# A decoder layer on one core: gaps of 128 and 256 bytes behind the two halves of the split activations

## The chip, the cores and the metric

One Trainium2 chip, one of its cores. The metric is the device time of one execution in microseconds; the time before is the median of three executions.

## The reference

One decoder layer on 256 tokens of width 2048, all in float32:

```
h = rms_norm(x); proj = h @ w_in                     # 2048 x 13312
o_da  = differential attention (8 heads), o_ret = retention (8 heads)
o_mem = cross-attention into 256 memory tokens (w_mem_kv: 2048 x 2048)
merged = sum_b sigmoid(gate_b) * (o_b @ w_o_b)       # 3 x 1024 x 2048
x = x + merged @ w_out                               # 2048 x 2048
hf = rms_norm(x)
x = x + (silu(hf @ w_ffn_gate) * (hf @ w_ffn_up)) @ w_ffn_down   # width 5632
```

## The kernel before, in words

Nearly all of the work is in matrix products, and each product runs as three passes on TensorE. Every float32 operand is split into a high part, rounded to the type fp32r, and a low part, the remainder, kept in fp32r too; the product is hi x hi, hi x lo and lo x hi, added up in PSUM. The activations are the stationary operand (a tile of 128 rows by 128 tokens, so 512 bytes in each partition), and the weights are the moving operand (512 columns, so 2048 bytes in each partition). For every pass the stationary tile is loaded anew, since TensorE's weight load belongs to each matmul. In the code:

```
for n, (a, w) in enumerate(((hi, w_hi), (hi, w_lo), (lo, w_hi))):
    e = pe.matmul(dst, a[:, k0 + k, tok], w[:, s % RING, k, :], ...)
```

That is line 1582 (`three_passes`), which the projections, the branches and the output projection use. Lines 1664 to 1666 (`product`) are the same three passes for the feed-forward part and for the blocks that run with seven products in place of eight.

The stationary tiles live in a few places:

- `hT_hi` and `hT_lo`, 16 x 256 float32 per partition (16,384 bytes each), hold the two halves of the transposed normed residual stream. They serve the input projection, the three branch gates, the gate and up projections of the feed-forward part, and, in four of their columns, its last down projection.
- `oT_hi` and `oT_lo`, as large, hold the memory tokens, then the branch outputs, then the merged rows.
- `aT_hi` and `aT_lo` hold the gated activations of a feed-forward block; `cmb_hi`, `cmb_lo`, `r_cmb` and `p_cmb` hold sums of activation blocks for the seven-product form.

The moving tiles are `w_hi` and `w_lo` (a ring of four slots), and in the feed-forward part `f_hi`, `f_raw` (whose remainder view is named `f_raw_rest`), and `sum`.

SBUF is handed out in the order of the declarations, each tensor right behind the one before it. Ahead of the activations stand the small tables, with a pad `align` of 32 bytes as the last of them. Then come `hT_hi`, `hT_lo`, `raw`, `w_hi`, `w_lo` and all other large tiles. Every size from `hT_hi` to the last is a multiple of 512 bytes per partition, so all these tiles start at one and the same place modulo 512: in the kernel before, the distance between any stationary tile and any moving tile that it meets is 0 modulo 512. The tile `ident`, the moving operand of the transposes (line 1604, `turn`), stands among the small tables; from it to `hT_hi` it is 256 bytes modulo 512.

The order of the work is written out by hand for each engine. SP loads the weights into `raw` or `f_raw`, ScalarE (line 507, and 847 to 857) makes the high part, VectorE (line 929, and 1427 to 1440) the low part, and TensorE multiplies. TensorE waits for semaphores that VectorE raises (`lo_done`, `part_lo`). TensorE's stream of passes is broken at some places by transposes and by the small attention products in plain float32 (lines 1642 and 1657, 128 x 256 moving columns).

Of the kernel before, what the change touches and what calls it, by code (L numbers as in the profile page):

```python
# [33 lines left out]
P = 128  # L34
# [28 lines left out]
UNIT_PART = (0, 1, 3, 5, 7, 8, 10, 12, 14, 15, 16, 17)  # L63
PARTS, UNITS, SLOTS, RAWS, SUMS, NS = 18, 12, 5, 5, 3, 6
ALIGN = 8
SUM_PART = (2, 4, 6, 9, 11, 13)
N0, S0W, S0T, S1W, S1T, S2W, S2T, N1, S3W, S3T, S4W, S4T, S5W, S5T, D0, D1, D2, D3 = range(PARTS)
RB_KIND = ("nnSnSnSn", "nSnSSnSn")
# [21 lines left out]
def program(nc, x, mem, positions, w_in, da_q_norm_g, da_k_norm_g, da_lambda_q1, da_lambda_k1,  # L90
# [6 lines left out]
    with ExitStack() as ctx:  # L97
        def sb(name, shape, dt=F32):
            return ctx.enter_context(nc.sbuf_tensor(name, shape, dt))
# [33 lines left out]
        lrden = sb("lrden", [P, 2, 2])  # L133
        sb("align", [P, ALIGN])
        hT_hi = sb("hT_hi", [P, KD, TOK], F32R)
        hT_lo = sb("hT_lo", [P, KD, TOK], F32R)


        with ExitStack() as mixers:
# [151 lines left out]
        def part(f, p):  # L291

            return (f - 1) * PARTS + p
# [626 lines left out]
        def _(v):  # L920
# [522 lines left out]
            def sum_first(f, i, u):  # L1443
# [4 lines left out]
                if (f - 1) * NS + i >= SUMS:  # L1448
                    e, j = divmod((f - 1) * NS + i - SUMS, NS)
                    v.wait_ge(part_done, part(e + 1, SUM_PART[j]) + 1)  # L1450
                elif i == 2:
# [583 lines left out]
```

## Time and profile before

| what | value |
|---|---|
| runs, median of three | 1628.27 us (1627.23 to 1629.32) |
| span of the profiled execution | 1625.4 us |
| TensorE matmul busy | 1618.2 us, 7373 matmuls |
| TensorE weight load busy | 1339.3 us, 7373 loads |
| VectorE busy | 1271.1 us |
| ScalarE busy | 908.2 us |
| granted TensorE clock | 1.000 (mean) |

The span runs from the first to the last instruction of the profiled execution; for that execution no other time is shown, and the runs' median lies 2.9 us above its span. Matmuls are pipelined, and the busy time of each (some 390 ns) overlaps that of the next, so what a matmul costs is the distance from its start to the next one's start; the chain of work that ended last gives it, as time divided by count.

### The profile page before, as it was taken

The numbers are of one execution on the slowest core, as the hardware profiler recorded it, in microseconds if no ns is written. First come the engines' busy times: TensorE is split into PE (matmuls) and PEld (weight loads), VectorE is DVE, ScalarE is ACT, GpSimd is POOL, SyncE is SP. The second block draws the span as 40 slices with busy tenths as digits, with TensorE's granted clock in tenths as the row PEclk, the third lists the DMA queues.
The fourth block names the chain that finished last, engine by engine and source line by source line (L and its number), as shares of the span: only waits on it lengthen the run. The fifth ranks groups of instructions, "written<-read, shape, count | busy, mean of one in ns | idle before, by whom it ended". The sixth has DMA issues, their size and how long they took to land.

```text
span 1625.4 us, 20227 instructions
## 1 busy us (share of the span) xinstructions
PE 1618.2 (100%) x7373; PEld 1339.3 (82%) x7373; DVE 1271.1 (78%) x1325; ACT 908.2 (56%) x989; POOL 80.6 (5%) x73
## 2 busy tenths in 40 slices
PE   9999999999999999999999999999999999999999
PEld 7888888888888888888888888888888888888887
DVE  5565545589777777777975589999999999999995
ACT  6654454555555554445554465656655665656653
POOL 0000000000011100000000000100100100100101
PEclk9999999999999999999999999999999999999999
DMA  9876555556554555566675756868868868868866
GB/s 339 278 214 194 157 180 175 174 179 220 179 166 162 164 172 168 174 188 199 202 245 182 249 166 207 252 211 248 246 212 250 249 208 249 244 220 240 253 211 178
DMA packets 178007, 341.35 MB, mean 210 GB/s; under 512 B 11793, under 2 KB 16401, under 8 KB 177169
## 3 DMA queue, kind: packets, MB, share of 16 engines
q1 hardware_dynamic: 167056, 319.45, 60.4%
q0 software_dynamic: 10880, 20.97, 7.1%
q8 instruction: 44, 0.72, 0.2%
q14 instruction: 27, 0.21, 0.0%
HBM read 317.31 MB, written 2.10 MB: 197 GB/s over the span
## 4 chain that ended last, share of the span: by engine, by line
PE 90%; issue 6%; DVE 1%; DMA 1%; POOL 1%; ACT 1%; SPq 0%; DVEq 0%; ACTq 0%; POOLq 0%
PE acc L1582 43%; PE at L1664 9%; PE at L1666 9%; PE at L1665 9%; PE acc L1666 5%; PE acc L1664 5%; PE acc L1665 5%; PE at L1582 3%; PE at L1604 2%; POOL rstd L480 1%; PE at L1642 0%; PE at L1657 0%; DMA raw<-in_w_mem_kv 0%; DMA raw<-in_w_in 0%; DVE w_lo L929 0%
## 5 line engine op out<-in xcount | busy, mean ns | idle before, releaser
L929 DVE TENSOR_TENSOR w_lo<-raw,w_hi 128x1024 fp32r<-128x1024 f32 x319 | 386.6, 1222 | 239.6 <-ACT w_hi L507 235.4
L507 ACT ACTIVATE w_hi<-raw 128x1024 fp32r<-128x1024 f32 x319 | 337.1, 1060 | 360.9 <-PE acc L1582 300.3
L1582 PE MATMUL acc<-w_hi,hT_hi 128*128 128x512 f32 x752 | 297.6, 396 | 0.0
L1582 PE MATMUL acc<-w_hi,hT_lo 128*128 128x512 f32 x752 | 293.1, 390 | 0.0
L1582 PE MATMUL acc<-w_lo,hT_hi 128*128 128x512 f32 x752 | 293.0, 390 | 0.0
L857 ACT ACTIVATE f_hi<-sum 128x2048 fp32r<-128x2048 f32 x60 | 115.3, 1922 | 121.2 <-DVE sum L1461 118.0
L1582 PEld LDWEIGHTS acc<-w_hi,hT_hi 128*128 128x128 f32 x752 | 141.2, 188 | 30.9 <-issue 1.3
L1582 PEld LDWEIGHTS acc<-w_hi,hT_lo 128*128 128x128 f32 x752 | 141.2, 188 | 29.7
L1582 PEld LDWEIGHTS acc<-w_lo,hT_hi 128*128 128x128 f32 x752 | 141.3, 188 | 28.4
L1582 PE MATMUL acc<-w_hi,oT_hi 128*128 128x512 f32 x384 | 151.2, 394 | 1.5 <-DVE oT_lo L955 1.4
L1582 PE MATMUL acc<-w_hi,oT_lo 128*128 128x512 f32 x384 | 149.6, 390 | 0.0
L1582 PE MATMUL acc<-w_lo,oT_hi 128*128 128x512 f32 x384 | 149.5, 389 | 0.0
L1427 DVE TENSOR_TENSOR f_raw_rest<-f_raw,f_hi 128x2048 fp32r<-128x2048 f32 x64 | 145.2, 2283 | 4.3 <-ACT f_hi L847 4.3
L1440 DVE TENSOR_TENSOR sum_rest<-sum,f_hi 128x2048 fp32r<-128x2048 f32 x60 | 137.2, 2286 | 3.9 <-ACT f_hi L857 3.9
L1664 PE MATMUL at<-f_hi,aT_hi 128*128 128x512 f32 x320 | 124.7, 390 | 0.1
L1666 PE MATMUL at<-f_hi,aT_lo 128*128 128x512 f32 x320 | 124.7, 390 | 0.0
L1665 PE MATMUL at<-f_raw_rest,aT_hi 128*128 128x512 f32 x320 | 124.6, 389 | 0.0
L847 ACT ACTIVATE f_hi<-f_raw 128x2048 fp32r<-128x2048 f32 x64 | 119.8, 1904 | 0.0
L1664 PE MATMUL acc<-f_hi,hT_hi 128*128 128x512 f32 x280 | 109.9, 393 | 0.0
L1666 PE MATMUL acc<-f_hi,hT_lo 128*128 128x512 f32 x280 | 109.1, 390 | 0.0
L1434 DVE TENSOR_TENSOR f_raw_rest<-f_raw,f_hi 128x1536 fp32r<-128x1536 f32 x60 | 105.2, 1753 | 0.7
L852 ACT ACTIVATE f_hi<-f_raw 128x1536 fp32r<-128x1536 f32 x60 | 88.9, 1481 | 12.6 <-PE acc L1666 9.7
(349 smaller groups left out, 2658.1 us busy)
## 6 DMA issues: line engine op xcount, KB each, us to landing
raw<-in_w_in SPq DMA_DIRECT2D x208, 512.0 KB, 3.8
f_raw<-in_w_ffn_down SPq DMA_DIRECT2D x88, 512.0 KB, 4.8
f_raw<-in_w_ffn_gate SPq DMA_DIRECT2D x80, 512.0 KB, 3.9
f_raw<-in_w_ffn_up SPq DMA_DIRECT2D x80, 512.0 KB, 5.0
proj<-down POOLq DMA_DIRECT2D x40, 512.0 KB, 6.4
raw<-in_w_mem_kv SPq DMA_DIRECT2D x32, 512.0 KB, 6.2
raw<-in_w_out SPq DMA_DIRECT2D x32, 512.0 KB, 3.7
raw<-in_w_o_mem SPq DMA_DIRECT2D x16, 512.0 KB, 5.0
```

The lines of the kernel that those rows point to most:

```text
L507: act.activation(w_hi[:, s % RING], raw[:, s % RING], ACT.Copy).then_inc(hi_done, 1)
L847: act.activation(f_hi[slot(f, p)][:], f_raw[unit(f, u) % RAWS][:], ACT.Copy).then_inc(part_hi, 1)
L852: act.activation(f_hi[slot(f, p)][:, 0:3], f_raw[unit(f, u) % RAWS][:, 1:4], ACT.Copy).then_inc(part_hi, 1)
L857: act.activation(f_hi[slot(f, p)][:], sums[sum_buf(f, i)][:], ACT.Copy).then_inc(part_hi, 1)
L929: v.tensor_tensor(w_lo[:, s % RING], raw[:, s % RING], w_hi[:, s % RING].bitcast(F32), ALU.subtract).then_inc(lo_done, 1)
L1427: v.tensor_tensor(f_rest[r][:], f_raw[r][:], f_hi[slot(f, p)][:].bitcast(F32), ALU.subtract).then_inc(part_lo, 1)
L1434: v.tensor_tensor(f_rest[r][:, 1:4], f_raw[r][:, 1:4], f_hi[slot(f, p)][:, 0:3].bitcast(F32), ALU.subtract).then_inc(part_lo, 1)
L1440: v.tensor_tensor(sums_rest[n][:], sums[n][:], f_hi[slot(f, p)][:].bitcast(F32), ALU.subtract).then_inc(part_lo, 1)
L1582: e = pe.matmul(dst, a[:, k0 + k, tok], w[:, s % RING, k, :], start=first and k == 0 and n == 0, stop=last and k == 1 and n == 2)
L1664: pe.matmul(dst, hi, whi, start=first, stop=False)
L1665: pe.matmul(dst, hi, wlo, start=False, stop=False)
L1666: return pe.matmul(dst, lo, whi, start=False, stop=last)
```

## The change

Two tensors that nothing reads or writes are declared behind `hT_hi` and behind `hT_lo`:

```
+HI_GAP, LO_GAP = 32, 64
...
         sb("align", [P, ALIGN])
         hT_hi = sb("hT_hi", [P, KD, TOK], F32R)
+        sb("hi_gap", [P, HI_GAP])
         hT_lo = sb("hT_lo", [P, KD, TOK], F32R)
+        sb("lo_gap", [P, LO_GAP])
```

They take 128 and 256 bytes in each partition. `hT_hi` stays where it was, `hT_lo` moves up by 128 bytes, and everything declared behind it by 384 bytes. No instruction is added, removed or moved on any engine.

## Rows read from the trace of the kernel before

**Rows 1.** The page: span, and busy time of each engine.
```profile
span 1625.4 us, 20227 instructions
PE 1618.2 (100%) x7373; PEld 1339.3 (82%) x7373; DVE 1271.1 (78%) x1325; ACT 908.2 (56%) x989; POOL 80.6 (5%) x73
PEclk9999999999999999999999999999999999999999
```
**Rows 2.** The page: chain that ended last; and TensorE's clock over the core.
```profile
PE 90%; issue 6%; DVE 1%; DMA 1%; POOL 1%; ACT 1%; SPq 0%; DVEq 0%; ACTq 0%; POOLq 0%
...
core 0: 1625.4 us, clock 1.000
```
**Rows 3.** The chain in order of time: start us, us, what, xcount.
```profile
19.92 70.27 PE acc L1582 x310
...
99.94 46.24 PE acc L1582 x204
...
157.04 1.73 PE at L1642 x8
...
174.59 24.50 PE acc L1582 x108
...
954.85 22.67 PE acc L1582 x100
```
**Rows 4.** Groups by line and tiles, TensorE: xcount | busy us, mean ns.
```profile
L1582 PE MATMUL acc<-w_hi,hT_hi 128*128 128x512 f32 x752 | 297.6, 396 | 0.0
L1582 PE MATMUL acc<-w_hi,oT_hi 128*128 128x512 f32 x384 | 151.2, 394 | 1.5 <-DVE oT_lo L955 1.4
L1664 PE MATMUL at<-f_hi,aT_hi 128*128 128x512 f32 x320 | 124.7, 390 | 0.1
L1664 PE MATMUL acc<-f_hi,hT_hi 128*128 128x512 f32 x280 | 109.9, 393 | 0.0
L1665 PE MATMUL acc<-f_raw_rest,hT_hi 128*128 128x512 f32 x220 | 85.6, 389 | 0.0
L1664 PE MATMUL at<-f_hi,cmb_hi 128*128 128x512 f32 x180 | 70.0, 389 | 0.0
L1664 PE MATMUL at<-f_hi,hT_hi 128*128 128x512 f32 x92 | 35.8, 389 | 0.0
L1665 PE MATMUL acc<-sum_rest,hT_hi 128*128 128x512 f32 x60 | 23.3, 389 | 0.0
L1582 PE MATMUL at<-w_hi,hT_hi 128*128 128x512 f32 x40 | 15.6, 389 | 0.0
L1664 PE MATMUL acc<-w_hi,hT_hi 128*128 128x512 f32 x13 | 5.1, 389 | 0.0
L1604 PE MATMUL at<-ident,proj 128*128 128x128 f32 x112 | 14.5, 272 | 0.0
```
**Rows 5.** Timeline of TensorE's weight loads: start us, us, what, xcount.
```profile
149.19 0.19 PEld L1582 LDWEIGHTS acc<-w_lo,hT_hi 128*128 128x128 f32 x1
149.42 0.19 PEld L1582 LDWEIGHTS acc<-w_hi,hT_lo 128*128 128x128 f32 x1
```
**Rows 6.** Timeline of the matmuls there, and behind the break.
```profile
148.96 0.39 PE L1582 MATMUL acc<-w_hi,hT_lo 128*128 128x512 f32 x1
149.19 0.39 PE L1582 MATMUL acc<-w_hi,hT_hi 128*128 128x512 f32 x1
149.41 0.39 PE L1582 MATMUL acc<-w_lo,hT_hi 128*128 128x512 f32 x1
...
151.66 0.40 PE L1582 MATMUL acc<-w_lo,hT_hi 128*128 128x512 f32 x1
151.89 0.39 PE L1582 MATMUL acc<-w_hi,hT_lo 128*128 128x512 f32 x1
152.12 0.39 PE L1582 MATMUL acc<-w_hi,hT_hi 128*128 128x512 f32 x1
152.35 0.39 PE L1582 MATMUL acc<-w_lo,hT_hi 128*128 128x512 f32 x1
```
**Rows 7.** Timeline of the matmuls at the start, behind a wait for weights.
```profile
11.59 0.50 PE L1582 MATMUL acc<-w_hi,oT_hi 128*128 128x512 f32 x1
11.93 0.40 PE L1582 MATMUL acc<-w_lo,oT_hi 128*128 128x512 f32 x1
12.17 0.40 PE L1582 MATMUL acc<-w_hi,oT_lo 128*128 128x512 f32 x1
...
13.80 0.40 PE L1582 MATMUL acc<-w_hi,oT_hi 128*128 128x512 f32 x1
```
**Rows 8.** Timeline in the feed-forward part: passes on `cmb`, between passes on `hT`.
```profile
1047.25 0.39 PE L1664 MATMUL acc<-f_hi,cmb_hi 128*128 128x512 f32 x1
...
1049.74 0.39 PE L1666 MATMUL at<-f_hi,cmb_lo 128*128 128x512 f32 x1
1049.97 0.39 PE L1664 MATMUL acc<-f_hi,hT_hi 128*128 128x512 f32 x1
```
**Rows 9.** Busy time by stretch: the feed-forward part, 1000 to 1100 us.
```profile
core 0: us, PE busy (x) PEld busy (x) DVE busy (x) ACT busy (x) POOL busy (x), PEclk, DMA share, GB/s
1000.00:1100.00 100.00, 100.00 (x446) 82.67 (x446) 94.81 (x72) 62.21 (x50) 8.50 (x7) 1.00 0.76 228
```

More of the change, by code:

```diff
@@ L65 @@
 ALIGN = 8
+HI_GAP, LO_GAP = 32, 64
 SUM_PART = (2, 4, 6, 9, 11, 13)
@@ L135, in program @@
         hT_hi = sb("hT_hi", [P, KD, TOK], F32R)
+        sb("hi_gap", [P, HI_GAP])
         hT_lo = sb("hT_lo", [P, KD, TOK], F32R)
+        sb("lo_gap", [P, LO_GAP])
         with ExitStack() as mixers:
```

## The prediction, made before the changed kernel ran

> **What bounds the kernel now.** I read the page's busy times first. TensorE's matmuls fill 1618.2 of 1625.4 us [rows 1]; the reader is to see that only TensorE can set the time. The chain that ended last says the same: 90% of it is matmuls, and the granted clock is 1.000, the upper of its two levels, 2.4 GHz [rows 2]. So the question is not who is waited for but how far apart two matmuls start. The chain in order of time answers that as time over count [rows 3]: 70.27 us for 310 passes from 19.92 us on is 226.7 ns, 46.24 us for 204 is 226.7 too, 24.50 us for 108 is 226.9, and 22.67 for 100 is 226.7. The first of these stretches has `oT` as the stationary operand (the memory projection), the other three have `hT`. A busy time of 390 ns [rows 4] is not that price, since the matmuls overlap.
>
> The same chain holds a comparison. The attention scores, 8 matmuls in plain float32 with 256 columns each, take 1.73 us, or 216 ns apiece [rows 3]. Their weight load reads 512 bytes a partition as well, and their operands are also 0 apart modulo 512. A pass of 512 columns at one column a cycle of 2.4 GHz would be 213.3 ns. So a pass costs 13.4 ns more than this, and 10.7 ns more than the small product. That 10.7 ns is what might hang on addresses, and it is the one quantity that this change could touch on the way that sets the time.
>
> Where could addresses come in? The timeline shows that the load of the next stationary tile starts with the pass before it: a load starts at 149.19 and another at 149.42 us [rows 5], and passes start at 149.19 and 149.41 [rows 6]. So two reads of SBUF by TensorE run side by side for each pass: 2048 bytes of moving weights and 512 bytes of stationary activations. That is where a collision would sit if there is one.
>
> **The change part by part.** It adds no instruction and takes none away; all terms are changes of the distance between two starts.
>
> First term, passes with `hT` stationary. The distance from the stationary to the moving tile goes from 0 to -128 modulo 512 for `hT_hi` (128 + 256 bytes lie between now), and from 0 to 256 for `hT_lo`. The count, from the groups [rows 4]: 752 triples in `acc` at line 1582 and 40 in `at`; in the feed-forward part and the seven-product blocks 280 + 92 first passes, as many third ones, and 220 + 60 + 92 second ones; with 13 + 13 triples of the retention gates, and some 13 triples more in small groups, it is 2,376 + 1,116 + 78 + 39 = 3,609, or about 3,600 passes of 6,800. Their price per pass is unknown, as the trace of before holds no pass at another distance modulo 512, so I bound it. Below: all 10.7 ns go, as in the small float32 product, 3,600 x 10.7 ns = 38.5 us gained. Above: the stream behind a break. There the passes of a triple start further apart for a while: from 11.93 to 13.80 us there are 8 steps, 234 ns each, 7 ns above the steady 226.7 [rows 7]; behind the transposes, from 151.66 to 152.35, 3 steps of 230 ns, 3.3 ns above it [rows 6]. So 3,600 x 7 = 25 us lost at most, and 12 us at the milder figure. Between these ends I take 0. The reason is in the two rows that are nearest. The small product has its two reads at distance 0 modulo 512 and pays nearly nothing, so distance 0 by itself is not what costs. And the four sums of a `cmb` block stand at four places modulo 2048, yet the 12 passes on them, from 1047.25 to 1049.97 us, start 226.7 ns apart like all others [rows 8]. What is dear is then the fp32r pass as such, not its place.
>
> Second term, passes with `oT`, `aT`, `cmb` and the like: both operands move by the same 384 bytes, the distance stays 0, and only the place itself changes. I put it at 0, between the same bounds per pass; there is no row that says a tile's own start matters, and a start at a multiple of 128 bytes stays one.
>
> Third term, the transposes: `ident` does not move, `proj`, `qn`, `pm` and `kvm` do, so their distance goes from 256 to 128 modulo 512. There are 112 on `proj` [rows 4] and some 300 in all. If each lost or won 10 ns it would be 3 us; I take 0, and leave the 3 us in the range.
>
> Fourth term, everything beside TensorE. VectorE is busy 94.81 us of 100 in the feed-forward part [rows 9]; its operands there all move together, so it stays as it is. DMA writes land 384 bytes further, in rows of 2 KB, still at multiples of 128 bytes. Cover for both is TensorE's busy stream: VectorE would have to slow by 5% there before it is late.
>
> Here two statements of the Trainium skill bear on it. The page "TensorE: Matmul & The Clock Gate" (section "Step-by-step: what each phase is for") says that TensorE has two independent read ports in SBUF, and that loading the next tile takes no read bandwidth from the running matmul. By that the first term is 0. The same page (section "Wait — 56ns, not 53.3ns?") gives 215.7 ns between warm matmuls of 512 columns; the trace disagrees, with 226.7 ns, so something does stretch the passes here. By its figure the passes could drop by 11 ns, an estimate of 40 us over the same count, which is the second rival below.
>
> **The sum** is 0: the profiled execution's span of 1625.4 us stays, and with it the median of the runs, 1628.3 us, which is 2.9 us above the span.
>
> **The rivals.** *The two reads collide, and the new distances loosen them: faster.* For it speaks that each pass costs 10.7 ns more than a float32 product with the same streaming time, and that the load starts together with the pass, so that at distance 0 both streams begin at the same place modulo 512. Against it, the float32 scores do the same and pay nothing. If both passes on `hT_hi` in a triple are freed and the one on `hT_lo` is not, it is two thirds: 2,400 x 10.7 = 26 us, 1602 us. If all are, 1590 us. VectorE caps it at 5% in the feed-forward part [rows 9], which is more than this asks.
>
> *The stream loses its lock: slower.* Behind a break the passes start 230 to 234 ns apart, then settle at 226.7 [rows 6, 7]; the steady value looks like a state that is reached when every pass meets its load in the same way. With the gaps a triple has unlike distances, -128, 256, -128, so the passes need not settle. The place is every triple on `hT`, some 1,200; the price is 3.3 to 7 ns a pass; that gives 1628.3 + 12 = 1640 us, at most 1653. It decides as soon as the distance of starts in a stretch of `hT` stays over 227.6 ns, since 0.9 ns a pass over 3,600 passes is 3.3 us, 0.2% of the time, about what a measurement of this kernel can tell from no change.
>
> *The change does nothing to the distances.* If the allocator rounded starts to 512 bytes the gaps would vanish or turn into whole steps. The kernel's own pad of 32 bytes, and tables of 8 and 24 bytes ahead of it, would then waste space; I find this unlikely, and its time is that of the forecast, so its chance goes with it.
>
> **How the numbers follow.** No change 0.46 (all forms of it, that of the idle gaps included), the loosened reads 0.27, the lost lock 0.27. The two rivals are alike in weight: the first has the 10.7 ns on its side, the second the slower starts behind breaks. The likeliest case gives 1628.3 us, by itself 1625 to 1632 (the transposes' 3 us on either side). The range takes in two thirds of the gain (1602) and the milder loss (1640) with some of the way to the greater: 1600 to 1645 us. Left out are the whole gain of 38 us, some 0.06, and a loss of over 17 us, some 0.08. The chances of faster, within 0.2% and slower are the same three: 0.27, 0.46, 0.27.
>
> **What the profile of the changed kernel would show.** If I am right, stretches of `hT` and of `oT` passes both stay at 226.7 to 227 ns, and behind breaks the same few slower starts. If the first rival is right, a stretch such as that of 204 passes from 99.94 us [rows 3] drops below 46 us, towards 44.1, while the feed-forward's `aT` passes stay. If the second is, that stretch grows to 46.9 us or more and its starts vary from pass to pass. What would prove me wrong in a way that I did not name: `oT` and `aT` passes, whose distance stays 0, change as well.

## The result, and the profile after

The changed kernel takes 1649.1 us (median of four executions, 1649.0 to 1650.7), the kernel before 1627.8 us beside it. The ratio is 1.0135, with a 95% interval of 1.0122 to 1.0147: slower by 1.35%, some 21.4 us between the medians. No change was forecast.

The page of the changed kernel, busy times and clock, and the chain that ended last:

```profile
span 1647.3 us, 20227 instructions
PE 1640.5 (100%) x7373; PEld 1341.0 (81%) x7373; DVE 1272.1 (77%) x1325; ACT 908.3 (55%) x989; POOL 80.7 (5%) x73
...
PEclk9999999999999999999999999999999999999999
...
PE 99%; DMA 0%; DVE 0%; ACT 0%; issue 0%
```

Against [rows 1] the reader is to see that the instruction counts are the same, the clock is granted as before, and VectorE and ScalarE are as busy as before within 1 us. TensorE's matmul time grew by 22.3 us, its weight loads by 1.7, and the span by 21.9. TensorE waits no more than before for anyone: 3.2 us in all, before 3.4. It does the same passes more slowly. (VectorE idles longer ahead of its `w_lo` pieces, 251.3 us against 239.6; it gets its slots later and is not the bound.)

That the chain is now 99% TensorE, against 90% in [rows 2], is no change of limit. In the kernel before, the chain left TensorE for one long piece, 97.27 us in which nothing was waited for that the profile shows:

```profile
350.16 97.27 issue
```

TensorE was busy for all of the time from 350 to 447 us there, as in the changed kernel.

The chain in order of time says which passes became slower (start us, us, what, count; `three_passes` is now at line 1585, `turn` at 1607, the scores at 1645):

```profile
19.97 70.04 PE acc L1585 x309
...
99.88 52.04 PE acc L1585 x223
...
158.38 1.73 PE at L1645 x8
...
881.22 21.78 PE acc L1585 x96
...
925.65 0.87 PE at L1607 x8
...
952.07 39.19 PE acc L1585 x168
```

The first row holds passes on `oT`: 70.04 / 309 = 226.7 ns, as in [rows 3]. So do the 96 passes from 881.22 us: 226.9 ns. The rows from 99.88 and 952.07 us hold passes on `hT`, and they take 52.04 / 223 = 233.4 ns and 39.19 / 168 = 233.3 ns, where [rows 3] had 226.7 to 226.9. The eight float32 scores take 1.73 us as before. Eight transposes take 0.87 us. In the kernel before, where the distance from `ident` to the source was 256 modulo 512 and not 128 as now, they took as long:

```profile
1039.69 0.87 PE at L1604 x8
```

A stretch of the timeline of the changed kernel, with `hT` as the stationary operand (start us, us, what):

```profile
120.26 0.39 PE L1585 MATMUL acc<-w_hi,hT_hi 128*128 128x512 f32 x1
120.49 0.40 PE L1585 MATMUL acc<-w_lo,hT_hi 128*128 128x512 f32 x1
120.72 0.40 PE L1585 MATMUL acc<-w_hi,hT_lo 128*128 128x512 f32 x1
120.96 0.39 PE L1585 MATMUL acc<-w_hi,hT_hi 128*128 128x512 f32 x1
...
121.66 0.39 PE L1585 MATMUL acc<-w_hi,hT_hi 128*128 128x512 f32 x1
```

Two triples, from 120.26 to 121.66 us, take 1.40 us, 233.3 ns a pass, and the pattern repeats: two steps of 0.23 and one of 0.24 us. This is no disturbance that dies away as it did behind the breaks in [rows 6, 7]; it is the steady state. The whole of it: about 3,600 passes by 6.6 ns is 23.8 us, against 21.9 us of span. The rest is in the first steps behind breaks, which were slow already: over the 41 breaks that passes on `hT` at this line follow, the second to fourth step average 232.3 ns before and 232.7 ns after.

### The profile page after: what moved, and what is told of

Same layout as the page of the kernel before. It is cut to its first block, busy times and chain, and to the rows that moved or that the text cites. A ratio compares the mean times of both kernels' runs of the same rounds, so it can differ in the third digit from the quotient of the medians.

```text
span 1647.3 us, 20227 instructions
## 1 busy us (share of the span) xinstructions
PE 1640.5 (100%) x7373; PEld 1341.0 (81%) x7373; DVE 1272.1 (77%) x1325; ACT 908.3 (55%) x989; POOL 80.7 (5%) x73
## 4 chain that ended last, share of the span: by engine, by line
PE 99%; DMA 0%; DVE 0%; ACT 0%; issue 0%
PE acc L1585 48%; PE at L1669 9%; PE at L1668 9%; PE at L1667 9%; PE acc L1668 5%; PE acc L1667 5%; PE acc L1669 5%; PE at L1585 4%; PE at L1607 2%; PE at L1660 0%; PE at L1645 0%; DMA raw<-in_w_mem_kv 0%; PE at L1741 0%; PE at L1739 0%; PE acc L1607 0%; PE at L1780 0%
## 5 line engine op out<-in xcount | busy, mean ns | idle before, releaser
L932 DVE TENSOR_TENSOR w_lo<-raw,w_hi 128x1024 fp32r<-128x1024 f32 x319 | 387.4, 1223 | 251.3 <-ACT w_hi L510 247.2
L1585 PE MATMUL acc<-w_hi,hT_lo 128*128 128x512 f32 x752 | 298.4, 397 | 0.0
L1585 PE MATMUL acc<-w_lo,hT_hi 128*128 128x512 f32 x752 | 297.1, 395 | 0.0
L855 ACT ACTIVATE f_hi<-f_raw 128x1536 fp32r<-128x1536 f32 x60 | 89.0, 1484 | 13.5 <-PE acc L1669 10.7
```

The costliest lines, as they stand in the source:

```text
L855: act.activation(f_hi[slot(f, p)][:, 0:3], f_raw[unit(f, u) % RAWS][:, 1:4], ACT.Copy).then_inc(part_hi, 1)
L932: v.tensor_tensor(w_lo[:, s % RING], raw[:, s % RING], w_hi[:, s % RING].bitcast(F32), ALU.subtract).then_inc(lo_done, 1)
```

## The experiments

All of them have the code of the changed kernel and other gaps. Each run's text from before it ran names its rival explanations as theories with a letter, and the paragraphs behind it say which of them fall. A step is the distance from one start to the next. A distance is that from the stationary tile up to the moving tile, in bytes, modulo the number that is said; "high" and "low" are `hT_hi` and `hT_lo`. The price is read in each trace from one stretch of the chain that starts at about 100 us and has `hT` throughout.

### First group: unlike distances, or a price for each distance?

The changed kernel has unlike distances for the two halves, which the forecast's slower rival blamed. So one run gives both halves 256, one gives both 128, and two mix 0 with 256.

**Both at 256.** Only the gap behind `hT_lo` stays:
```
-        sb("hi_gap", [P, HI_GAP])
```


> One gap of 256 bytes behind hT_lo alone: both halves stand 256 from the weights modulo 512. Theory A (unlike distances of the two halves keep the stream from settling): the distances are alike again, so passes on hT settle at 226.7 ns and the time is that of before, 1628 us. Theory B (each distance has a price of its own, and only 0 is cheap): 256 is not cheap, passes on hT start 233 ns apart or more, 1650 to 1657 us.

Measured: 1628.3 us, ratio 1.0004 (0.9993 to 1.0015).
```profile
99.91 46.24 PE acc L1584 x204
```
46.24 / 204 is 226.7 ns, the value of before, over the same count as in [rows 3].

**Both at 128.**
```
-HI_GAP, LO_GAP = 32, 64
+HI_GAP, LO_GAP = 0, 32       # and no hi_gap
```


> One gap of 128 bytes behind hT_lo alone: both halves stand 128 from the weights. Theory A: 226.7 ns, 1628 us. Theory B: a price of its own, 232 to 235 ns per pass on hT, 1645 to 1655 us; if the price comes with the sign of the distance (the changed kernel has -128 for the high half), it may also be a gain.

Measured: 1649.0 us, ratio 1.0134 (1.0104 to 1.0163).
```profile
99.89 46.24 PE acc L1584 x199
```
That is 232.4 ns a pass, with alike distances.

**High at 0, low at 256.**
```
-HI_GAP, LO_GAP = 32, 64
+HI_GAP, LO_GAP = 64, 64
```


> Gaps of 256 and 256 bytes: the high half stands 512, so 0 modulo 512, from the weights, the low half 256. Theory A: unlike distances, slower as in the changed kernel, 1640 to 1650 us, and all three steps of a triple longer. Theory B: only the step at which the low half is loaded or used pays, one in three: about 7 us, 1635 us, the other steps 226.7 ns.

Measured: 1627.2 us, ratio 0.9999 (0.9988 to 1.0011).
```profile
99.79 46.24 PE acc L1585 x204
```

**High at 256, low at 0.**
```
-HI_GAP, LO_GAP = 32, 64
+HI_GAP, LO_GAP = 64, 0       # and no lo_gap
```


> One gap of 256 bytes between the halves: the high half stands 256 from the weights, the low half 0. Theory A: unlike distances, slower, 1640 to 1650 us. Theory B: two steps of three pay, about 14 us, 1642 us, and the step of the low half stays 226.7 ns.

Measured: 1628.0 us, ratio 1.0005 (0.9994 to 1.0016).
```profile
99.84 46.24 PE acc L1584 x204
```

What follows: theory A falls in both directions. Unlike distances (0 and 256) cost nothing, and alike ones (128 and 128) cost as much as the whole change. Theory B falls too as it was put, since 256 has no price. In all that was tried 256 is as good as 0. So I take it that what counts is the distance modulo 256, not modulo 512 as the change's own words have it; between 256 and 512 only 384 was run, in the high half of the changed kernel. Seen so, the changed kernel has its high half at 128 and its low half at 0.

### Second group: which half, and what other distances cost

**High at 0, low at 128 (modulo 256).** The mirror of the changed kernel:
```
-HI_GAP, LO_GAP = 32, 64
+HI_GAP, LO_GAP = 32, 32
```


> Gaps of 128 and 128 bytes: the high half stands 256, so 0 modulo 256, from the weights, the low half 128; the changed kernel has it the other way round (128 and 0 modulo 256). Theory C (a distance of 128 modulo 256 costs, at the loads or passes that have it): one step of three pays instead of two, about 1628 + 7 to 11 us, 1635 to 1639 us. Theory D (any mixture or any distance off 0 keeps the stream from settling): all steps longer, as in the changed kernel, 1645 to 1650 us.

Measured: 1641.4 us, ratio 1.0086 (1.0057 to 1.0115).
```profile
99.92 46.22 PE acc L1585 x200
```
231.1 ns on average, and its timeline shows how the triple divides:
```profile
119.86 0.39 PE L1585 MATMUL acc<-w_hi,hT_hi 128*128 128x512 f32 x1
120.09 0.40 PE L1585 MATMUL acc<-w_lo,hT_hi 128*128 128x512 f32 x1
120.32 0.40 PE L1585 MATMUL acc<-w_hi,hT_lo 128*128 128x512 f32 x1
120.56 0.39 PE L1585 MATMUL acc<-w_hi,hT_hi 128*128 128x512 f32 x1
...
121.25 0.39 PE L1585 MATMUL acc<-w_hi,hT_hi 128*128 128x512 f32 x1
```
Of the four starts that stand here the steps are 0.23, 0.23 and 0.24 us. With the trace's nanoseconds, averaged over the kernel, the step from `w_hi`,`hT_hi` to `w_lo`,`hT_hi` takes 227.1 ns, the one that ends with the first pass on `hT_lo` 232.5, and the next one, behind the pass on `hT_lo`, 233.8. So it is neither "one in three pays" nor "all pay": one tile at a bad distance makes two steps long, that in which it is loaded and that in which it is used. Theory C had the tile right, but it expected one long step in three and 7 to 11 us; two are long, and 14 us are lost. Theory D, all steps longer and 1645 us or more, falls.

**Both at 64, 192 and 32.** One gap behind `hT_lo`, for 64 bytes:
```
-HI_GAP, LO_GAP = 32, 64
+HI_GAP, LO_GAP = 0, 16       # 48 for 192 bytes, 8 for 32; no hi_gap
```


> One gap of 64 bytes behind hT_lo: both halves 64 from the weights. Theory C with a price that grows with the distance from 0 up to 128: between 1628 and 1649 us, near 1638. Theory D: 1645 us or more. Theory E (some other distance holds the two reads clear of each other): below 1628 us, down to 1590.

> One gap of 192 bytes behind hT_lo: both halves 192, so -64 modulo 256, from the weights. Theory C, if only the size of the distance counts: as with 64 bytes. If the sign counts (weights behind or ahead of the load), it differs from the run with 64 bytes, and one of the two may lie below 1628 us, down to 1590 (theory E).

> One gap of 32 bytes behind hT_lo: both halves 32 from the weights; the tiles from raw on then start at 416 modulo 512, no longer at a multiple of 64 bytes. Theory C: a small price, 1628 to 1635 us. Theory D: 1645 us. Theory E: below 1628 us.

Measured: 1634.7 us with 64 (ratio 1.0044, 1.0024 to 1.0064), 1649.8 us with 192 (1.0137, 1.0108 to 1.0167), 1648.6 us with 32 (1.0130, 1.0101 to 1.0160). The same stretch in the three kernels, in that order:
```profile
99.88 46.24 PE acc L1584 x202
```
```profile
99.87 46.20 PE acc L1584 x198
```
```profile
99.85 46.20 PE acc L1584 x198
```
These are 228.9, 233.3 and 233.3 ns. A price that grows with the distance falls (32 costs 6.6 ns, 64 only 2.2), and so does one that depends on its size alone (64 and 192 are the same size with opposite signs).

### Third group: the other distances, and which pair of tiles it is

**Both at 96, 160 and 224.** As above, with `LO_GAP` = 24, 40 and 56.

> One gap of 96 bytes behind hT_lo, both halves 96 from the weights. So far 0 and 256 give 226.7 ns per pass on hT, 32 gives 233.3, 64 gives 229.1, 128 gives 232.5, 192 gives 233.3. Theory I (0 is the best place, all others cost, in no order that follows the distance): 228 to 234 ns, 1632 to 1652 us. Theory E (some distance is cheaper than 0): below 226.7 ns, below 1627 us.

> One gap of 160 bytes behind hT_lo, both halves 160 from the weights. Theory I: 228 to 234 ns per pass on hT, 1632 to 1652 us. Theory E: below 226.7 ns, below 1627 us.

> One gap of 224 bytes behind hT_lo, both halves 224, so -32 modulo 256, from the weights. Theory I: 228 to 234 ns per pass on hT, 1632 to 1652 us. Theory E: below 226.7 ns, below 1627 us.

Measured: 1653.8 us with 96 (ratio 1.0160, 1.0131 to 1.0190), 1653.9 us with 160 (1.0161, 1.0132 to 1.0191), 1650.3 us with 224 (1.0139, 1.0110 to 1.0169). In that order:
```profile
99.85 46.20 PE acc L1584 x198
```
```profile
99.88 46.16 PE acc L1584 x197
```
```profile
99.88 46.20 PE acc L1584 x198
```

| distance modulo 256, both halves | ns a pass on `hT` in the stretch | time, us |
|---|---|---|
| 0 (before; 256) | 226.7 | 1627.2; 1628.3 |
| 32 | 233.3 | 1648.6 |
| 64 | 228.9 | 1634.7 |
| 96 | 233.3 | 1653.8 |
| 128 | 232.4 | 1649.0 |
| 160 | 234.3 | 1653.9 |
| 192 | 233.3 | 1649.8 |
| 224 | 233.3 | 1650.3 |

Theory E, a distance cheaper than 0, finds nothing in steps of 32 bytes. Theory I stands: 0 is the best of eight. No version beats the kernel before. The last column is no mere multiple of the middle one. The groups of 12 passes on `cmb`, which stand between passes on `hT`, grow as well, though their own distance is 0. From the traces' starts, all 60 groups together take 163.2 us before, 2.7 us more with 128, 2.9 with 96, 1.8 with 160, 1.7 with 224, 0.8 with 192, and 0.5 or less with 32 and 64. That is a part of the difference between 96 and 224, not all of it.

**The pairs matched.** Which two reads are it that meet? In the run with the low half at 128, `w_lo` is moved by 128 bytes as well:
```
             w_hi = mixer("w_hi", [P, RING, 2, NCOL], F32R)
+            mixer("w_gap", [P, 32])
             w_lo = mixer("w_lo", [P, RING, 2, NCOL], F32R)
+            mixer("w_gap2", [P, 32])
...
-            ..., ("f_hi4", quad_tile, F32R), ("f_raw4", quad_tile, F32), ...
+            ..., ("f_hi4", quad_tile, F32R), ("f_gap", [P, 64], F32), ("f_raw4", quad_tile, F32), ...
```
The last line keeps the feed-forward's tiles off `oT`, 256 bytes further, so at the same place modulo 256.

> The run with the low half of the activations at 128 (gaps of 128 and 128 bytes), and now w_lo too is 128 bytes further, with 128 more behind it, so oT stays at 0 from w_hi and stands at 128 from w_lo. So hT_hi and w_hi are at 0, hT_lo and w_lo at 128. Theory G (what counts is the load of the next stationary tile against the moving tile of the pass in flight): at line 1582 hT_lo is loaded while w_lo streams, and hT_hi while w_hi streams, so all loads stand at 0 and all three steps fall back to 226.7 ns, while on oT the step with w_lo in flight grows to 232.5 and the one behind it to 234. Feed-forward as in the run with the low half at 128. 1641.4 - 10.6 + 5.8 = 1637 us. Theory H (what counts is a pass's own stationary tile against its own moving tile): the passes w_lo x hT_hi and w_hi x hT_lo stand at 128 and stay long, 232 to 234 ns, 1641 to 1647 us.

Measured: 1647.1 us, ratio 1.0120 (1.0090 to 1.0149). The chain, first a stretch on `oT`, then one on `hT`:
```profile
19.88 70.23 PE acc L1587 x301
```
```profile
99.90 46.23 PE acc L1587 x200
```
`oT`, at 0 from `w_hi` and 128 from `w_lo`, now costs 233.3 ns a pass. No step of an `oT` triple stays at 226.7 any more; they take 236, 234 and 230 ns in the trace:
```profile
40.25 0.40 PE L1587 MATMUL acc<-w_hi,oT_hi 128*128 128x512 f32 x1
40.49 0.40 PE L1587 MATMUL acc<-w_lo,oT_hi 128*128 128x512 f32 x1
40.72 0.39 PE L1587 MATMUL acc<-w_hi,oT_lo 128*128 128x512 f32 x1
40.95 0.40 PE L1587 MATMUL acc<-w_hi,oT_hi 128*128 128x512 f32 x1
```
The longest step is the first, 0.24 us. There `w_hi` is in flight and `oT_hi`, at 0 from it, is loaded, while the pass that follows has `w_lo`, at 128. `hT` stands at 231.2 ns, the value of the run without this edit, although every load there now is at 0 from the tile in flight. Theory G, the load against the pass in flight and nothing else, falls: it wanted 226.7 ns on `hT` and 1637 us. Theory H said 232 to 234 ns for two steps of three and 1641 to 1647 us; the time agrees at its edge, but on `hT` the steps repeat only after two triples, with 236, 235, 234, 224, 232 and 226 ns at one place, which theory H does not give. Both pairs of tiles seem to count, and what a step costs depends on the one before it. How, stays open.

**Is it another engine?** The gaps also move `hT` against what VectorE and ScalarE read and write. The traces separate this. In the changed kernel, from 100 to 146 us, the 128 steps in which VectorE works average 233.5 ns and the 68 in which it does not 233.1; for ScalarE it is 233.5 and 233.2. In the kernel before, all four are 226.6 or 226.7 ns. In the run with the matched pairs, the `oT` steps from 20 to 90 us average 233.1 ns with VectorE at work and 233.8 without. So the steps are long with those engines idle too. The landing of the weights in `raw` was not separated in this way; but in the run with the matched pairs `oT` became dear although `raw` stayed at 0 modulo 256 from it.

## Why the prediction was wrong

**What held.** The bound: TensorE's stream sets the time, and no other engine came into it; VectorE is busy 1272.1 us against 1271.1. The second, third and fourth terms were put at 0. The third is confirmed by the rows of the transposes above: from 0 to 128 modulo 256, and no slower. The second is confirmed too: in every run without a gap behind `w_hi`, passes on `oT` stay at 226.7 ns in the stretch from 20 to 90 us, with both tiles 32 to 512 bytes further than in the kernel before, so a tile's own start is of no account among those tried. The count of 3,600 passes was right (the trace has 3,609), and the price lay within its bounds: these were 10.7 ns gained and 7 ns lost, and 6.6 ns were lost.

**The step that failed** is the choice within the first term: "Between these ends I take 0. The reason is in the two rows that are nearest." Both rows have distance 0 modulo 256, and so has every pass in the trace of before; even the transposes, at 256 modulo 512, are at 0 modulo 256. From "distance 0 pays little in float32" I took that distance does not matter. The runs show the reverse reading: distance 0 is the cheapest of eight places, and the passes of before already had it everywhere. The 10.7 ns by which such a pass is dearer than the float32 product did not hang on the distance; they stayed at distance 0, and at the others 2.2 to 7.6 ns came on top. The float32 product was a poor stand-in in two more ways. That its 256 columns stream as long as the 512 of a pass was assumed, and no run shows it. And plain float32 need not answer to the distance as fp32r does: the transposes on `proj` start 108.8 to 109.1 ns apart in every run, at all eight distances modulo 256. The `cmb` row was weaker still: its four places differ by multiples of 512 bytes, which are 0 modulo 256, so it could not tell anything.

**The range** ended at 1645 us, short of the 1649.1. It took in only "the milder loss" of 12 us with some of the way to the greater, and weighed a loss of over 17 us at 0.08. The upper bound that stood in the text, 25 us, would have held the time.

**The slower rival** (0.27) had the time, 1640 us and at most 1653, the place, and its point of decision: the stretch from about 100 us rose above 227.6 ns, to 233.4. Its mechanism, unlike distances that keep the stream from settling, did not hold: 0 and 256 mixed cost nothing, 128 for both costs as much as the change. What can be kept of it is what the starts behind breaks showed: that a pass's length depends on how it meets its neighbours was there in [rows 6, 7], with prices of 3.3 and 7 ns, and I weighed it too low. That its price of 3.3 to 7 ns encloses the 6.6 is luck: it was read from steps behind breaks, which are long at distance 0 too, and the steady price comes with the distance and not with a break. **The faster rival** fell with all eight distances.

**The rule that I set beside the first term** was that of the Trainium skill, "TensorE: Matmul & The Clock Gate", section "Step-by-step: what each phase is for": that loading the next tile takes no read bandwidth from the running matmul. The runs disagree with what I drew from it, a term of 0: with the same instructions and clock, the distance of the two tiles alone moves a pass from 226.7 to as much as 234.3 ns. The 215.7 ns that the same page of the Trainium skill gives between warm matmuls of 512 columns (section "Wait — 56ns, not 53.3ns?") was reached at none of the eight distances; the lowest is 226.7 ns.

## What to carry to other kernels

Where TensorE's stream of fp32r passes with a fresh stationary tile each is the bound, keep stationary and moving tiles at one place modulo 256 bytes, the best of the places in steps of 32 bytes that were tried here; a table or a pad of 32 to 224 bytes that is declared between them cost up to 1.6% of this whole kernel with no wait to be seen in the profile. Look for it as time over count in the chain, not as busy time or as a wait. And a trace in which a quantity has one value throughout says nothing of other values: then the middle of the bounds is no better founded than the ends, and the range has to reach them.

## What the runs showed of the hardware that was not expected

- The distance between the stationary and the moving tile matters in fp32r passes, and 256 is as good as 0: 226.7 ns a pass at 0 and at 256, 232.4 at 128. The float32 transposes (128 moving columns) stay at 109 ns at every distance tried.
- It is not monotonic and not symmetric: 64 costs 2.2 ns, 32, 96, 192 and 224 cost 6.6 ns, 160 costs 7.6.
- The stream falls into a repeating pattern of steps, and a tile at 128 lengthens also the step behind it (233.8 ns at distance 0, behind a pass at 128, in the run with only the low half off). Passes on `cmb`, at distance 0 themselves but between passes on `hT`, grow with `hT` at 128: 60 groups of 12 take 165.9 us in place of 163.2.
- Even at distance 0 such a pass takes 13.4 ns more than 512 columns at one a cycle of 2.4 GHz would. What makes up these was not tried.
